# Down projection with GpSimd's transfers adding up the wide weight sum of each seven-product group

## The chip, the cores and the metric

The kernel runs on one core of one Trainium2 chip. The metric is the device time of one execution in microseconds (us), less is better. The core has TensorE (PE, matrix products into PSUM), VectorE (DVE), ScalarE (ACT), GpSimd (POOL) and SyncE (SP); SP and POOL also issue transfers between HBM and SBUF, and all transfers share 16 DMA engines.

## The reference, cut to what matters

One decoder layer on 256 tokens of width 2048: a mixing block, then a SwiGLU feed-forward block, then a final RMSNorm. The change lies in the last product, `w_down`.

```
D_MODEL = 2048
SEQ = 256
D_FF = -(-8 * D_MODEL // 768) * 256      # 5632
...
    hf = rms_norm(x, norm_ffn)
    gate, up = jnp.split(hf @ w_gu, 2, axis=-1)
    return x + (jax.nn.silu(gate) * up) @ w_down
...
    return rms_norm(x, norm_final)
```

Everything is float32.

## The kernel before, in words

**Products in three parts.** A float32 weight tile is taken as a high part (`w_hi`, rounded by ACT to the format TensorE multiplies) and a low part (`w_lo`, the rest, by DVE). Activations are kept as `actT_hi` and `actT_lo` in the same way. Each product of 128 rows by 512 columns is then three matmuls: high by high, high by low, low by high.

**The down projection.** The 5632 rows of `w_down` are 22 blocks `k` of 256 rows (`UPD`), the 2048 columns are two halves, each of a left and a right column group of 512 (`GW`). The 256 tokens are two blocks of 128. The list `DOWN`, made by `down_order()`, says in which order a half's 22 blocks are worked. A block goes in one of two ways:

- a **pair**: one unit for the left columns, one for the right. A unit is 2 token blocks by 2 row chunks by 3 matmuls, so 12 matmuls, and a pair 24;
- a **seven**: seven products of sums of the four parts of the activations with sums of the four parts of the weights stand for the eight, so 21 matmuls. It takes four slots of `w_hi` and `w_lo`: the left weights (2 products), one row chunk of the right weights (1 product), the **wide weight sum** (2 products, 1024 columns wide) and the second sum, which DVE adds up in `act_tok` from the wide one (2 products).

`SUMMED` (9) blocks of each half are sevens, those with even `k`; the others are pairs between them. The last two blocks of half 0 and the last three (`LAST`) of half 1 are worked as all their left units, then all their right units.

**Slots and who waits for whom.** `raw` (the loaded weights), `w_hi` and `w_lo` have `R` = 4 slots each. SP loads into a slot of `raw` once DVE has made the low part of what stood there (`lo_ready`). ACT writes a slot of `w_hi` once PE has used the unit four slots earlier (`unit_used`), DVE then writes the same slot of `w_lo`, and PE starts the unit at `lo_ready`. Every engine works its own list strictly in order; the order of `DOWN` sets them all.

**Names that the prediction uses.** On DVE: `down_low` makes `w_lo` from `raw` (L1269), `sum_low` makes it from a sum (L1275); `weight_sums` makes the wide sum in `gate_s` (L1287, 128x1024) and then the second sum in two steps (L1291, L1293, 128x512); `act_low` (L1096) finishes the last activations. After the last seven of a half, `fold_banks` (L1313 to L1320) and `fold_sums` (L1326 to L1328) add the banks of the shared products into the residual `x1`: `fold_banks` waits until PE is done with that seven, and is called behind the low part of the second item after it (`after == 2`), `fold_sums` behind that of the third. At the start of half 1, `down_add` (L1257) adds the two left banks of half 0 ahead of the low part of the seven's second slot, and the two right banks behind the low part of its wide sum; PE may not start that seven's third product (`product(2, s4, ...)`) before the first of the two right banks has been added (`residual_added`).

On POOL: after the last feed-forward unit it loads the kept residual back (L430, `x_kept`, 2 transfers of 1024 KB) and the row of the final norm (L431, `nf_row`, 1024 KB).

## Time and profile before

| | |
|---|---|
| median of 3 runs | 1103.7 us (1103.67 to 1104.84) |
| profiled execution, its own time | 1104.13 us |
| its span in the trace | 1102.4 us |
| TensorE busy | 1090.8 us, 99% of the span |
| VectorE busy | 863.6 us, 78% |
| ScalarE busy | 580.9 us, 53% |
| GpSimd busy | 41.3 us, 4% |
| chain that ended last | PE 96%, DVE 2%, issue 1%, DMA 1% |
| moved by DMA | 215.31 MB, mean 195 GB/s |

The trace's span begins at the first recorded instruction and leaves out what lies around it; that is the difference between the span and the execution's own time. The down projection lies between about 865 us and the end. A matmul's row shows 0.39 us, but matmuls are pipelined and start one behind another in less than that, so their pace is read from the start times.

### The profile page before, as it was taken

Reading aid. Unit: us, or ns where it says so; the run is one execution under the profiler, and the core shown is the slowest. Engines: PE = TensorE matmul, PEld = TensorE weight load, DVE = VectorE, ACT = ScalarE, POOL = GpSimd, SP = SyncE. Lnnn points to the kernel's source line nnn. Section 1 sums busy time; section 2 is a strip of 40 time slices with the busy share of each in tenths; the row PEclk is TensorE's granted clock in tenths of the full one; section 3 lists DMA queues with packets and bytes.
Section 4 is the critical chain, followed back from the end, with each engine's and each line's share of the span. In section 5 each row is a group of like instructions: output and inputs, shape, how many; then the busy total and the mean of one; then the engine's idle time right before and its main releaser. Section 6 shows DMA issues by size and latency. Waiting matters only on the chain.

```text
span 1102.4 us, 13887 instructions
## 1 busy us (share of the span) xinstructions
PE 1090.8 (99%) x5097; PEld 907.1 (82%) x5097; DVE 863.6 (78%) x1059; ACT 580.9 (53%) x704; POOL 41.3 (4%) x68
## 2 busy tenths in 40 slices
PE   9999999999999999999999999999999999999997
PEld 7797889888888888888888888888888888888885
DVE  5556866688756557988988889889888899899896
ACT  5655545555545444645545545446455556546553
POOL 2600000000010000000000000000000000000000
PEclk9999999999999999999999999999999999999999
DMA  8665646565546575656557557566566766666663
GB/s 283 212 201 171 179 134 180 160 172 153 187 176 224 178 263 175 211 170 213 197 162 230 165 177 241 173 194 209 170 212 194 282 206 213 199 199 210 201 224 115
DMA packets 110925, 215.31 MB, mean 195 GB/s; under 512 B 6940, under 2 KB 11616, under 8 KB 109984
## 3 DMA queue, kind: packets, MB, share of 16 engines
q1 hardware_dynamic: 108960, 205.36, 59.3%
q0 software_dynamic: 1632, 8.96, 2.2%
q8 instruction: 28, 0.46, 0.2%
q10 hardware_dynamic: 288, 0.39, 0.1%
q14 instruction: 17, 0.14, 0.0%
HBM read 210.49 MB, written 4.19 MB: 195 GB/s over the span
## 4 chain that ended last, share of the span: by engine, by line
PE 96%; DVE 2%; issue 1%; DMA 1%; ACT 0%; SPq 0%; POOLq 0%; POOL 0%; ACTq 0%; DVEq 0%
PE acc L1398 11%; PE acc L1400 11%; PE acc L1399 11%; PE acc L1669 11%; PE acc L1670 11%; PE acc L1671 11%; PE acc L1734 5%; PE acc L1735 5%; PE acc L1736 5%; PE mx L1390 2%; PE mx L1669 2%; PE mx L1670 2%; PE mx L1671 2%; PE mx L1734 1%; PE mx L1735 1%; PE mx L1736 1%
## 5 line engine op out<-in xcount | busy, mean ns | idle before, releaser
L749 DVE TENSOR_TENSOR w_lo<-raw,w_hi 128x1024 fp32r<-128x1024 f32 (+2 forms) x144 | 166.5, 1168 | 119.0 <-ACT w_hi L450 118.3
L450 ACT ACTIVATE w_hi<-raw 128x1024 fp32r<-128x1024 f32 (+2 forms) x144 | 144.5, 1014 | 136.1 <-PE acc L1400 130.9
L638 ACT ACTIVATE w_hi<-raw 128x1024 fp32r<-128x1024 f32 (+1 forms) x160 | 158.5, 1005 | 96.2 <-PE acc L1671 78.6
L1669 PE MATMUL acc<-w_hi,hT_hi 128*128 128x512 f32 x520 | 203.4, 391 | 0.0
L1169 DVE TENSOR_TENSOR w_lo<-raw,w_hi 128x1024 fp32r<-128x1024 f32 (+1 forms) x160 | 180.6, 1155 | 29.0 <-ACT w_hi L638 27.2
L1670 PE MATMUL acc<-w_lo,hT_hi 128*128 128x512 f32 x520 | 202.4, 389 | 0.0
L1671 PE MATMUL acc<-w_hi,hT_lo 128*128 128x512 f32 x520 | 202.3, 389 | 0.0
L1398 PE MATMUL acc<-w_hi,hT_hi 128*128 128x512 f32 (+2 forms) x444 | 169.1, 381 | 0.4 <-DVE w_lo L749 0.4
L1400 PE MATMUL acc<-w_hi,hT_lo 128*128 128x512 f32 (+2 forms) x444 | 166.4, 375 | 0.0
L1399 PE MATMUL acc<-w_lo,hT_hi 128*128 128x512 f32 (+2 forms) x444 | 166.3, 375 | 0.0
L1671 PEld LDWEIGHTS acc<-w_hi,hT_lo 128*128 128x128 f32 x520 | 97.6, 188 | 20.5
L1669 PEld LDWEIGHTS acc<-w_hi,hT_hi 128*128 128x128 f32 x520 | 97.6, 188 | 20.1
L1670 PEld LDWEIGHTS acc<-w_lo,hT_hi 128*128 128x128 f32 x520 | 97.7, 188 | 20.0
L682 ACT ACTIVATE w_hi<-raw 128x1024 fp32r<-128x1024 f32 x88 | 83.2, 969 | 34.1 <-PE acc L1736 25.5
L1269 DVE TENSOR_TENSOR w_lo<-raw,w_hi 128x1024 fp32r<-128x1024 f32 x88 | 94.5, 1111 | 6.0 <-ACT w_hi L682 3.9
L1736 PE MATMUL acc<-w_hi,actT_lo 128*128 128x512 f32 x250 | 97.3, 389 | 0.0
L1398 PEld LDWEIGHTS acc<-w_hi,hT_hi 128*128 128x128 f32 x444 | 83.4, 188 | 16.1 <-issue 0.9
L1400 PEld LDWEIGHTS acc<-w_hi,hT_lo 128*128 128x128 f32 x444 | 83.4, 188 | 15.2
L1399 PEld LDWEIGHTS acc<-w_lo,hT_hi 128*128 128x128 f32 x444 | 83.4, 188 | 14.0
L1734 PE MATMUL acc<-w_hi,actT_hi 128*128 128x512 f32 x232 | 90.5, 390 | 0.0
L1735 PE MATMUL acc<-w_lo,actT_hi 128*128 128x512 f32 x232 | 90.3, 389 | 0.0
L644 ACT ACTIVATE w_hi<-ff_sum 128x1024 fp32r<-128x1024 f32 x40 | 42.5, 1063 | 74.6 <-PE acc L1671 59.6
(296 smaller groups left out, 1512.5 us busy)
## 6 DMA issues: line engine op xcount, KB each, us to landing
raw<-in_w_gu SPq DMA_DIRECT2D x176, 512.0 KB, 4.1
raw<-in_w_down SPq DMA_DIRECT2D x88, 512.0 KB, 4.6
raw<-in_w_in SPq DMA_DIRECT2D x80, 512.0 KB, 3.9
raw<-in_w_out SPq DMA_DIRECT2D x32, 512.0 KB, 4.2
raw<-in_w_in SPq DMA_DIRECT2D x8, 272.0 KB, 2.9
raw<-in_w_in SPq DMA_DIRECT2D x8, 264.0 KB, 2.8
x<-in_x POOLq DMA_DIRECT2D x2, 1024.0 KB, 7.5
x_kept<-x POOLq DMA_DIRECT2D x2, 1024.0 KB, 6.5
```

The costliest lines, as they stand in the source:

```text
L638: act.activation(w_hi[:, v % R, c0:UC * GW], raw[:, i % R, c0:UC * GW], ACT.Copy).then_inc(hi_ready, 1)
L749: dve.tensor_tensor(w_lo[:, slot, 0:UC * width], raw[:, slot, 0:UC * width], w_hi[:, slot, 0:UC * width].bitcast(F32), ALU.subtract).then_ ...
L1169: dve.tensor_tensor(w_lo[:, v % R, c0:UC * GW], raw[:, i % R, c0:UC * GW], w_hi[:, v % R, c0:UC * GW].bitcast(F32), ALU.subtract).then_inc ...
L1398: pe.matmul(o, hi[:, c + i, tb], wh, start=first and i == 0, stop=False)
L1399: pe.matmul(o, hi[:, c + i, tb], wl, start=False, stop=False)
L1400: ins = pe.matmul(o, lo[:, c + i, tb], wh, start=False, stop=last and i == UC - 1)
L1669: pe.matmul(o, a[0], w[0], start=first, stop=False)
L1670: pe.matmul(o, a[0], w[1], start=False, stop=False)
L1671: return pe.matmul(o, a[1], w[0], start=False, stop=last)
L1734: pe.matmul(o, a[0], w[0], start=first, stop=False)
L1735: pe.matmul(o, a[0], w[1], start=False, stop=False)
L1736: return pe.matmul(o, a[1], w[0], start=False, stop=last)
```

## The change

Four things change together.

1. The wide weight sum is no longer made by DVE. `column_sums(i)` on POOL issues two plain transfers of one row chunk of the right columns into both halves of a tile, waits for them, and issues two accumulating transfers which add the left columns and the other row chunk onto them (4 transfers of 256 KB for each seven). Two tiles (`junk_f`, `gate_s`) take turns. The sum for seven `i` may begin when DVE has made the low part of the wide sum of seven `i - 2`; DVE's `weight_sums` of seven `i` waits for `d_summed`. The first two sums are issued ahead of the residual and the norm row.
2. The sums that can be made by adding alone have the right columns' sign turned, so the right columns' results are accumulated negated: ACT writes their high part with a scale of -1, DVE their low part with one scalar_tensor_tensor (`negated_low`), and the additions into the residual become subtractions.
3. Ten blocks of each half are sevens, not nine. At one place in each half (`ADJACENT`) two sevens follow each other with no pair between, and the pair between the last seven and the single units is gone in half 0 (in half 1 one of two pairs).
4. Of a seven's right weights only the row chunk that is used is loaded into `raw` (`load_lower`, 256 KB for 512 KB). The scratch of the squares and of the folds moves to `up_s`; `ident` moves behind the other tiles.

```diff
-SUMMED = 9
+SUMMED = 10
+ADJACENT = (6, 5)
...
-        between = odd[len(lead):len(lead) + SUMMED - 1]
+        between = odd[len(lead):len(lead) + 8]
...
             groups.append(("seven", 2 * i))
-            if i < SUMMED - 1:
-                groups.append(("pair", between[i]))
+            if i != ADJACENT[half] and between:
+                groups.append(("pair", between.pop(0)))
...
+            def load_lower(n, k, q):
+                sp.wait_ge(lo_ready, SLOT_OF.get(q - R, V_DN + q - R - U_DN) + 1)
+                sp.dma_start(raw[:, q % R, GW:2 * GW],
+                             w_down[(UC * k + 1) * P:(UC * k + 2) * P, n * GW:(n + 1) * GW]).then_inc(loaded[q % R], 16)
...
+            def column_sums(i):
+
+                half, k = SUM_GROUPS[i][0:2]
+                rows = [w_down[(UC * k + r) * P:(UC * k + r + 1) * P, :] for r in range(UC)]
+                left, right = (slice((2 * half + c) * GW, (2 * half + c + 1) * GW) for c in range(2))
+                tile = sum_tile(i)
+                for c in range(2):
+                    pool.dma_start(tile[:, c, :], rows[0][:, right]).then_inc(sem("d_loaded"), 16)
+                pool.wait_ge(sem("d_loaded"), 32 * (i + 1))
+                for c, src in enumerate((rows[0][:, left], rows[1][:, right])):
+                    pool.dma_start(tile[:, c, :], src, accum_op=ALU.add).then_inc(sem(f"d_summed{i % 2}"), 16)
+
             pool.wait_ge(unit_used, V_DN)
+            column_sums(0)
+            pool.wait_ge(sem("act_ready"), 2 * NG_FF)
+            column_sums(1)
             pool.wait_ge(sem("gate_used"), 2 * NG_FF)
             pool.wait_ge(sem("x1_stored"), 16 * NB)
             for b in range(NB):
                 pool.dma_start(x1[:, b, :], x1_kept[b * P:(b + 1) * P, :]).then_inc(sem("x1_back"), 16)
             pool.dma_start(nf_row[:, :], norm_final.partition_broadcast(P)).then_inc(sem("nf_loaded"), 16)
+            for i in range(2, len(SUM_GROUPS)):
+                pool.wait_ge(lo_ready, SUM_GROUPS[i - 2][2] + 3)
+                column_sums(i)
...
+            def negated_low(v, q):
+
+                dve.wait_ge(hi_ready, v + 1)
+                dve.scalar_tensor_tensor(out=w_lo[:, v % R, :], in0=raw[:, q % R, :], scalar=-1.0,
+                                         in1=w_hi[:, v % R, :].bitcast(F32), op0=ALU.mult, op1=ALU.subtract)\
+                   .then_inc(lo_ready, 1)
...
-                dve.tensor_tensor(gate_s[:, :, :], raw[:, a + 1, :].rearrange("p (k n) -> p k n", k=UC),
-                                  raw[:, a:a + 2, 0:GW], ALU.subtract).then_inc(sem("w_sums"), 1)
-                dve.wait_ge(sem("actT_psum"), NG_FF)
-                dve.wait_ge(sem("w_sums"), made - 1)
-                step(dve.tensor_tensor(act_tok[:, 0, :], raw[:, a + 1, GW:2 * GW], gate_s[:, 0, :], ALU.subtract))
+                dve.wait_ge(sem(f"d_summed{i % 2}"), 32 * (i // 2 + 1))
+                step(dve.tensor_tensor(act_tok[:, 0, :], raw[:, a + 1, GW:2 * GW], d[:, 0, :], ALU.add))
                 settle()
-                dve.tensor_tensor(act_tok[:, 1, :], raw[:, a, GW:2 * GW], act_tok[:, 0, :], ALU.subtract)\
+                dve.tensor_tensor(act_tok[:, 1, :], raw[:, a, GW:2 * GW], act_tok[:, 0, :], ALU.add)\
                    .then_inc(sem("w_sums"), 1)
...
             with dve.Fori(2, SUMMED + 1) as j:
                 gate_up(j)
-            gate_up(SUMMED + 1, summed=False)
```

How DVE's list changes at the turn from half 0 to half 1. Before, from the low part of the last seven's second sum up to the first seven of half 1 and its four `down_add`:

```order
457 L1275 TENSOR_TENSOR w_lo<-act_tok,w_hi 128x1024
458 L1269 TENSOR_TENSOR w_lo<-raw,w_hi 128x1024 x3
459 L1313 COPY gate_s<-mx 128x512
...
465 L1269 TENSOR_TENSOR w_lo<-raw,w_hi 128x1024
466 L1326 TENSOR_TENSOR x<-x,gate_s 128x512
...
469 L1269 TENSOR_TENSOR w_lo<-raw,w_hi 128x1024 x2
470 L1287 TENSOR_TENSOR gate_s<-raw 128x1024
471 L1291 TENSOR_TENSOR act_tok<-raw,gate_s 128x512
...
474 L1257 TENSOR_TENSOR x<-acc,x 128x512 x2
```

And of the change, from the first step of `fold_banks` (L1351) on; ahead of it stand two low parts, not three:

```order
436 L1351 COPY up_s<-mx 128x512
...
442 L1308 SCALAR_TENSOR_TENSOR w_lo<-raw,w_hi 128x1024
443 L1364 TENSOR_TENSOR x<-x,up_s 128x512
...
446 L1308 SCALAR_TENSOR_TENSOR w_lo<-raw,w_hi 128x1024
447 L1327 TENSOR_TENSOR act_tok<-raw,junk_f 128x512
448 L1329 TENSOR_TENSOR act_tok<-raw,act_tok 128x512
449 L1302 TENSOR_TENSOR w_lo<-raw,w_hi 128x1024
450 L1289 TENSOR_TENSOR x<-x,acc 128x512 x2
451 L1302 TENSOR_TENSOR w_lo<-raw,w_hi 128x512
452 L1315 TENSOR_TENSOR w_lo<-junk_f,w_hi 128x1024
453 L1289 TENSOR_TENSOR x<-x,acc 128x512 x2
```

Between the folds and the seven there is one low part less and no wide subtraction; PE has four units to work there, not six.

Where two sevens follow each other (shown in half 0), DVE's list in the change has the second sum of the later seven right behind the last low part of the earlier:

```order
493 L1315 TENSOR_TENSOR w_lo<-gate_s,w_hi 128x1024
494 L1315 TENSOR_TENSOR w_lo<-act_tok,w_hi 128x1024
495 L1327 TENSOR_TENSOR act_tok<-raw,junk_f 128x512
496 L1329 TENSOR_TENSOR act_tok<-raw,act_tok 128x512
497 L1302 TENSOR_TENSOR w_lo<-raw,w_hi 128x1024
498 L1302 TENSOR_TENSOR w_lo<-raw,w_hi 128x512
```

Before, two low parts of a pair stood between the second and the third of these rows at every seven.

POOL's list in the change, from the residual's storing on; before, L457's and L458's transfers followed it directly:

```order
63 L436 DMA x_kept<-x 128x2048 x2
64 L445 DMA junk_f<-in_w_down 128x512 x2
65 L448 DMA junk_f<-in_w_down 128x512 x2
66 L445 DMA gate_s<-in_w_down 128x512 x2
67 L448 DMA gate_s<-in_w_down 128x512 x2
68 L457 DMA x<-x_kept 128x2048 x2
69 L458 DMA nf_row<-in_norm_final 128x2048
70 L445 DMA junk_f<-in_w_down 128x512 x2
71 L448 DMA junk_f<-in_w_down 128x512 x2
```

Eight transfers are put ahead of the three old ones, and the third seven's sum stands behind them.

## Rows read from the trace of the kernel before

**Rows 1.** The page's busy times: busy us, share, instructions.

```profile
PE 1090.8 (99%) x5097; PEld 907.1 (82%) x5097; DVE 863.6 (78%) x1059; ACT 580.9 (53%) x704; POOL 41.3 (4%) x68
```

**Rows 2.** Everything PE waited for: us in total, times, longest.

```profile
PE acc L1441 <- POOL ident L359: 1.6, 1, 1.6
PE mx L1390 <- DMA tok<-in_x: 1.1, 1, 1.1
PE acc L1398 <- DVE w_lo L749: 0.4, 1, 0.4
PE acc L1734 <- DVE x L1257: 0.3, 1, 0.3
```

**Rows 3.** Windows: length, busy us of PE, PEld, DVE, ACT, POOL; clock, DMA share, GB/s.

```profile
870.00:876.00 6.00, 6.00 (x32) 5.08 (x31) 5.86 (x8) 3.55 (x4) 0.00 (x0) 1.00 1.01 419
876.00:960.00 84.00, 84.00 (x371) 69.15 (x371) 76.78 (x81) 49.36 (x55) 0.00 (x0) 1.00 0.65 211
```

**Rows 4.** PE's timeline (start, us): first matmuls of two pairs, one seven between.

```profile
984.53 0.39 PE L1734 MATMUL acc<-w_hi,actT_hi 128*128 128x512 f32 x1
...
994.73 0.39 PE L1734 MATMUL acc<-w_hi,actT_hi 128*128 128x512 f32 x1
```

**Rows 5.** POOL's timeline when the down projection begins.

```profile
865.42 1.06 POOL L430 DMA_DIRECT2D x<-x_kept  x2 [463.45 <-PE acc L1671]
```

**Rows 6.** DVE's timeline ahead of the first seven, and a wide scalar_tensor_tensor (grouped).

```profile
871.63 1.22 DVE L1287 TENSOR_TENSOR gate_s<-raw 128x1024 f32<-128x1024 f32 x1
872.95 0.69 DVE L1291 TENSOR_TENSOR act_tok<-raw,gate_s 128x512 f32<-128x512 f32 x1
...
874.28 1.22 DVE L1096 TENSOR_TENSOR actT_lo<-mx,actT_hi 128x1024 fp32r<-128x1024 f32 x1
875.42 1.82 DVE L1269 TENSOR_TENSOR w_lo<-raw,w_hi 128x1024 fp32r<-128x1024 f32 x2
...
L953 DVE SCALAR_TENSOR_TENSOR qT<-gwork,qT 96x1024 f32<-96x1024 f32 x1 | 1.2, 1215 | 0.0
```

**Rows 7.** PE's timeline: first matmul of the first seven.

```profile
876.95 0.39 PE L1734 MATMUL mx<-w_hi,actT_hi 128*128 128x512 f32 x1
```

**Rows 8.** DMA issues: count, KB each, median us from issue to landing.

```profile
raw<-in_w_down SPq DMA_DIRECT2D x88, 512.0 KB, 4.6
...
x_kept<-x POOLq DMA_DIRECT2D x2, 1024.0 KB, 6.5
...
nf_row<-in_norm_final POOLq DMA_DIRECT2D x1, 1024.0 KB, 12.5
...
x<-in_sgu_w POOLq DMA_DIRECT2D x1, 256.0 KB, 4.0
```

**Rows 9.** DVE's timeline at the turn of the halves.

```profile
964.96 0.68 DVE L1313 COPY gate_s<-mx 128x512 f32<-128x512 f32 x1
...
971.86 2.36 DVE L1269 TENSOR_TENSOR w_lo<-raw,w_hi 128x1024 fp32r<-128x1024 f32 x2
974.14 1.22 DVE L1287 TENSOR_TENSOR gate_s<-raw 128x1024 f32<-128x1024 f32 x1
...
980.86 1.28 DVE L1257 TENSOR_TENSOR x<-acc,x 128x512 f32<-128x512 f32 x2
```

**Rows 10.** PE's timeline at the turn of the halves.

```profile
963.59 0.39 PE L1734 MATMUL acc<-w_hi,actT_hi 128*128 128x512 f32 x1
...
981.05 0.39 PE L1736 MATMUL acc<-w_hi,actT_lo 128*128 128x512 f32 x1
981.69 0.47 PE L1734 MATMUL acc<-w_hi,s_hi 128*128 128x512 f32 x1 [0.26 <-DVE x L1257]
```

**Rows 11.** ACT's timeline at the turn of the halves.

```profile
963.85 1.06 ACT L682 ACTIVATE w_hi<-raw 128x1024 fp32r<-128x1024 f32 x1 [0.30 <-PE acc L1736]
```

**Rows 12.** PE's timeline: first matmul of the second seven of half 1.

```profile
990.65 0.39 PE L1734 MATMUL mx<-w_hi,actT_hi 128*128 128x512 f32 x1
```

**Rows 13.** DVE's timeline: low parts of that seven's wide and second sums.

```profile
989.86 1.22 DVE L1275 TENSOR_TENSOR w_lo<-gate_s,w_hi 128x1024 fp32r<-128x1024 f32 x1
992.00 1.23 DVE L1275 TENSOR_TENSOR w_lo<-act_tok,w_hi 128x1024 fp32r<-128x1024 f32 x1 [0.92 <-ACT w_hi L688]
```

**Rows 14.** DVE's groups from 870 us on: the wide subtractions (mean ns; idle before).

```profile
L1287 DVE TENSOR_TENSOR gate_s<-raw 128x1024 f32<-128x1024 f32 x18 | 22.0, 1220 | 1.2 <-DMA raw<-in_w_down 1.2
```

More of the change, by code:

```diff
@@ L123 @@
 LAST_SEVEN = [max(i for i, d in enumerate(DOWN) if d[0] == "seven" and d[1] == h) for h in range(2)]
+SUM_GROUPS = [(d[1], d[2], d[4]) for d in DOWN if d[0] == "seven"]
 FIRST_RIGHT = [i for i, d in enumerate(DOWN) if d[1] == 1][0]
@@ L203, in hybrid_layer @@
         early.close()
-        late = ExitStack()
-        actT_hi = sb("actT_hi", [P, FC, T], F32R, late, align=1024)
-        actT_lo = sb("actT_lo", [P, FC, T], F32R, late, align=1024)
-        gate_s = sb("gate_s", [P, NB, GW], where=late)
-        act_tok = sb("act_tok", [P, NB, GW], where=late)
-        s_lo = sb("s_lo", [P, SUMMED, 2, P], F32R, late, align=512)
-        up_s = sb("up_s", [P, NB, GW], where=late)
-        late.close()
         plain = ExitStack()
@@ L220, in hybrid_layer @@
         plain.close()
+        actT_hi = sb("actT_hi", [P, FC, T], F32R, align=1024)
+        actT_lo = sb("actT_lo", [P, FC, T], F32R, align=1024)
+        gate_s = sb("gate_s", [P, NB, GW])
+        act_tok = sb("act_tok", [P, NB, GW])
+        s_lo = sb("s_lo", [P, SUMMED, 2, P], F32R, align=512)
+        up_s = sb("up_s", [P, NB, GW])
+        ident = sb("ident", [P, P])
         xin = tok[:, :, :].rearrange("p b n -> p (b n)")[:, 0:NB * D].rearrange("p (b n) -> p b n", b=NB)
@@ L242, in a21, with sum_tile @@
             return t[:, 0:4 * SUMMED, :].rearrange("p (g c) t -> p g c t", c=4)[:, g0:g1, 0, P:2 * P]
+        junk_sq = up_s[:, 0, :]
+        def sum_tile(i):
+            return junk_f[:, :].rearrange("p (c n) -> p c n", c=2) if i % 2 == 0 else gate_s
         def summands(g0, g1):
@@ L669, in down_square @@
                 act.wait_ge(sem("residual_added"), 2 * NG_OUT + 2 * n + b + 1)
-                act.activation(junk_f[:, 0:GW], x1[:, b, n * GW:(n + 1) * GW], ACT.Square,
+                act.activation(junk_sq, x1[:, b, n * GW:(n + 1) * GW], ACT.Square,
                                accum_out=ss_f[:, b * NG_DN + n:b * NG_DN + n + 1]).then_inc(sem("f_squared"), 1)
@@ L676, in down_squares, with down_high, sum_high @@
                     down_square(n, b)
-            def down_high(v, q, c0=0):
+            def down_high(v, q, c0=0, sign=1.0):
                 act.wait_ge(loaded[q % R], 16 * (q // R + 1))
                 act.wait_ge(unit_used, v - R + 1)
-                act.activation(w_hi[:, v % R, c0:UC * GW], raw[:, q % R, c0:UC * GW], ACT.Copy).then_inc(hi_ready, 1)
-            def sum_high(v, src, made):
-                act.wait_ge(sem("w_sums"), made)
+                act.activation(w_hi[:, v % R, c0:UC * GW], raw[:, q % R, c0:UC * GW], ACT.Copy, scale=sign)\
+                   .then_inc(hi_ready, 1)
+            def sum_high(v, src, made, count):
+                act.wait_ge(made, count)
                 act.wait_ge(unit_used, v - R + 1)
@@ L698, in _ @@
             for i, (kind, half, k, q, v) in enumerate(DOWN):
-                down_high(v, q)
+                down_high(v, q, sign=-1.0 if kind == "right" else 1.0)
                 if kind == "pair":
-                    down_high(v + 1, q + 1)
+                    down_high(v + 1, q + 1, sign=-1.0)
                 if kind == "seven":
@@ L704, in _ @@
                     down_high(v + 1, q + 1, GW)
-                    sum_high(v + 2, gate_s, 2 * sevens - 1)
-                    sum_high(v + 3, act_tok, 2 * sevens)
+                    sum_high(v + 2, sum_tile(sevens - 1), sem(f"d_summed{(sevens - 1) % 2}"), 32 * ((sevens + 1) // 2))
+                    sum_high(v + 3, act_tok, sem("w_sums"), sevens)
                 if i in SPLIT_AT:
@@ L1335, in _ @@
                     if sevens > 1:
-                        weight_sums(q, 2 * sevens, earlier)
+                        weight_sums(q, sevens - 1, earlier)
                     earlier = v
-                down_low(v, q)
+                if kind == "right":
+                    negated_low(v, q)
+                else:
+                    down_low(v, q)
                 if kind == "pair":
@@ L1341, in _ @@
                         activate_folded(NG_FF - 1, V_DN)
-                    down_low(v + 1, q + 1)
+                    negated_low(v + 1, q + 1)
                 if kind == "seven":
@@ L1347, in _ @@
                     down_low(v + 1, q + 1, GW)
-                    sum_low(v + 2, gate_s)
+                    sum_low(v + 2, sum_tile(sevens - 1))
                     if i == FIRST_RIGHT:
@@ L1355, in _ @@
                 if i == 1:
-                    weight_sums(q + 2, 2, None)
+                    weight_sums(q + 2, 0, None)
                     act_low(NG_FF, 4 * (NG_FF - 1))
```

38 lines of the change are left out of this document (22 added, 16 removed).

## The prediction

> **What bounds the kernel now.** I read the page's busy times first: TensorE is busy for 1090.8 of 1102.4 us, VectorE for 78% [rows 1]. The list of what PE waited for says how much a relieved helper could give back: four waits, three before the down projection, and one of 0.3 us in it, for a residual addition by DVE [rows 2]. Cut into windows, the down projection shows PE without a gap from 876 to 960 us at full granted clock, with DVE busy 76.8 of 84 us and the DMA engines 65% busy at 211 GB/s [rows 3]. So DVE is nearly full but ahead, and only three things can move the time: the number of matmuls, their pace, and new waits of PE. The pace comes from two starts: from one pair to the next, with a seven between, 45 matmuls start in 994.73 - 984.53 = 10.20 us, 0.2267 us each [rows 4]. A pair is 5.44 us, a seven 4.76 us, a single unit 2.72 us.
>
> **What is taken out.** One more block in each half goes as a seven: 3 matmuls fewer, twice, so 6 x 0.2267 = **-1.36 us**. The wide subtractions leave DVE, 18 of 1.22 us, 22 us in all [rows 14]. I count them at nothing: PE did not wait for them. In their place weight_sums waits for a transfer. The negated low parts cost what the old ones did: a scalar_tensor_tensor of 1024 columns took 1.215 us, beside 1.22 us [rows 6]. ACT's scale adds no instruction. The tenth block's activation sums are DVE work in the last feed-forward group, as in the eight groups before it, where PE never waited.
>
> **What is moved: the turn of the halves.** Let T be PE's start on the first unit after half 0's last seven; before, T = 963.59 [rows 10]. Before, six units and the seven's first two products follow, so PE is due at its third product at T + 17.68 = 981.27; it starts at 981.69, 0.42 late, because DVE's first addition of a right bank began at 980.86 and released it 0.83 later [rows 9, 10]. Now four units lie there: due at T + 4 x 2.72 + 1.36 = T + 12.24. DVE's chain to the same addition begins with fold_banks, which cannot start before PE has left the last seven; ACT was released from that at T + 0.26 [rows 11]. From fold_banks to the addition DVE took 980.86 - 964.96 = 15.90 us. Of that go one low part (971.86 to 974.14 for two, so 1.14 [rows 9]) and the wide subtraction (871.63 to 872.95, 1.32 [rows 6]): 13.44 us. The third product starts at T + 0.26 + 13.44 + 0.83 = T + 14.53, 2.29 late where it was 0.42 late: **+1.87 us**. This holds any smaller wait of right unit 21 ahead of it, since DVE's chain is the longer. Behind the waiting matmul stands PE's whole list; nothing gives the time back. In half 1 a pair is still between seven and single units, which is half 0's old shape less one unit; DVE's low parts stay ahead there, and the tail is untouched.
>
> **Two sevens in a row.** DVE writes the second sum into act_tok, which it shares by all sevens, so it can begin for the later seven only behind the low part of the earlier's second sum. That started at 992.00 for a seven that PE began at 990.65, 1.35 after it, because ACT waits there for a slot, not because DVE was late [rows 12, 13]. Then: this low part 1.14, the two narrow additions 1.33 (872.95 to 874.28 [rows 6]), the next low part 1.22: 5.04 us after the seven's start, where PE is due after 4.76. 0.28 late, twice: **+0.56 us**. Before, 5.44 us of a pair lay between.
>
> **The new wait: is the first sum there in time?** POOL was released at 865.42 [rows 5] and would issue the first sum then. A POOL transfer takes 0.53 to issue (1.06 for two [rows 5]). DVE's chain from the old start of weight_sums was 1.32 + 1.33, act_low 1.14 (874.28 to 875.42), low part 1.22, end 876.64, and PE started at 876.95 [rows 6, 7]. Without the wide subtraction, weight_sums may start as late as 876.95 - 1.33 - 1.14 - 1.22 = 873.26, so the sum must land within **7.8 us**. It is two transfer pairs one behind the other. The trace has no accumulating transfer and no plain pair of 256 KB. One plain POOL transfer of 256 KB landed 4.0 us after issue, a pair of 1024 KB in 6.5 [rows 8]. For the accumulating pair the lower end is the plain one (4.0), the upper twice it (8.0); nothing suggests less, as the same bytes come from HBM. I take 4.0 and one more pass over the pair's 0.52 MB at the 419 GB/s that the full queues showed [rows 3], 5.2. Then 0.53 + 4.0 + 0.53 + 5.2 = 10.3, the sum is there at 875.7, PE starts at 875.7 + 1.33 + 1.14 + 1.22 = 879.4: **+2.4 us**. At the ends: 9.1 us, +1.2; and 13.1 us, +5.2.
>
> The Trainium skill ("DMA: Bandwidth & Descriptors", section on the SWDGE path) gives about 2.0 us plus bytes / 436 GB/s per POOL transfer. By it the pair of 1024 KB would take 6.8, and the trace agrees with 6.5; the single 256 KB would take 2.6, the row says 4.0. By the page a pair of 256 KB takes 3.2 and the sum 2 x 3.2 + 1.06 = 7.5 us, just in time, and this term is nil. The same page (rules for kernel authors) says that an accumulating transfer reads its destination and writes it later, which no run here has shown yet; it speaks for my extra pass.
>
> **Queued behind it.** The second sum is issued at about 871 and due 10.2 us of PE after the first: hidden. Then come x_kept's return and nf_row, which once took 12.5 us to land [rows 8]; issued at 878.2 now, landed at 890.7. Their own users come much later (folds near 960). But the third sum's loads stand behind them in POOL's queue: landed near 892.0, accumulated by 897.7. Due: PE reaches the third seven at 876.95 + 20.4 + 2.4 = 899.8, less 2.6 for sum and low part, 897.2. **+0.5 us**, at the ends 0 and 3. Later sums: tile free 0.4 after a seven's start (989.86 + 1.22, against 990.65 [rows 12, 13]), needed two periods of 10.2 later less 2.6: 17.4 us for 10.3. Around two sevens in a row 12 us: still hidden at 10.3, about 1 us late each at 13.1.
>
> **Traffic.** For each seven and pair the loads were 2.10 MB in 10.2 us, 206 GB/s, as the row says (211 [rows 3]). Now 1.84 for raw and 1.05 for the sums: 283 GB/s, or 334 if accumulating reads twice, against 419 when full. SP's loads (4.6 us to landing [rows 8]) may lengthen, but DVE frees their slots earlier than before by its 1.3 us per seven. Nil, with an end of +2.
>
> **The sum.** -1.36 + 1.87 + 0.56 + 2.4 + 0.5 = **+4.0 us**. The profiled execution took 1104.13, 0.4 above the median of the three runs; on the median this makes **1107.7 us**.
>
> **Rivals.**
> - *The first sums come in time* (within about 8.5 us). For it: the page's formula, and the pair of 1024 KB at 6.5. Against: 4.0 for a single 256 KB, and two dependent steps. Then -1.36 + 1.87 + 0.56 = +1.1, **1104.8**, no measurable change. It decides at a column sum of 8.9 us: above that the whole is over +2.2.
> - *The sums are late at every seven.* An accumulating transfer far slower than twice a plain one, so that a sum takes over 17.4 us. At 19 us it is 1.6 x 18 later, with 10 at the start: about **1140**. For it: no row shows such a transfer. Against: bytes and engines have room.
> - *PE's pace quickens when DVE has less to do.* 1% on 996 matmuls is -2.3 us: with sums in time 1102.5, and if the turn did not stall at all (-1.87 - 0.42) 1100.2. It would have to come to over 1.5% alone, or with the turn. Against: the pace of 0.2267 was read where DVE is as full as elsewhere, and no row ties the two. This is the faster side.
> - *DVE's relief pays.* It would have to be in waits of PE, and there were 0.3 us.
>
> **How the numbers follow.** No change is told from a change up to about 0.2% here (2.2 us). My forecast, with the turn, the neighbours and late first sums: 0.62, slower. Sums in time: 0.29, same. Late everywhere: 0.06, slower. Faster pace: 0.03. The range goes down to just under the second case, 1104.3, and up to where an accumulating pair of nearly 8 us puts it (+1.1 + 5.2 + 3 = +9.3): 1113.0.
>
> **What would show it.** PE's waits should now name DVE at four places: near 877 (its releaser a DMA into junk_f behind it, some 2.4 us), near 897, at the turn (2 us, the same addition of x) and at the two neighbouring sevens (0.3 each). A column sum from its first issue to landing near 10 us. Six matmuls fewer. If PE has no wait near 877, the sum was quick; if the turn shows under 1 us, the chain from fold_banks is not what releases it.

## The result, and the profile after

The change takes **1146.6 us** (median of 4 runs, 1146.0 to 1150.6) against 1103.8 before: ratio 1.0394, interval 1.0369 to 1.0418. The forecast was 1107.7 (1104.3 to 1113.0): the sign was right, the size wrong by more than a factor of ten. The case that I had given 0.06, sums late at every seven with about 1140 us, is the nearest in time; only part of its mechanism came, as shown below.

The page: busy times, two DMA queues of the whole run, and the engines' shares of the chain that ended last.

```profile
PE 1105.5 (97%) x5091; PEld 913.9 (80%) x5091; DVE 849.9 (74%) x1054; ACT 583.7 (51%) x708; POOL 99.8 (9%) x148
q1 hardware_dynamic: 106400, 200.12, 55.0%
q0 software_dynamic: 10592, 29.94, 10.4%
PE 77%; DMA 13%; DVE 6%; issue 1%; POOL 1%; ACT 1%; SPq 0%; POOLq 0%; DVEq 0%; ACTq 0%
```

Six matmuls fewer than in [rows 1], as forecast, and yet PE is busy 14.7 us longer; and the chain, 1% DMA before, is now 13% DMA. What PE waited for (us in total, times, longest), the down projection's two rows:

```profile
PE mx L1775 <- DVE w_lo L1302: 24.4, 11, 4.8
PE acc L1775 <- DVE x L1289: 1.7, 1, 1.7
```

26.1 us of waits where [rows 2] had 0.3. With the 14.7 us of busy time they make 40.5 of the span's 41.8 us (1144.2 - 1102.4). Windows of the down projection (columns as in [rows 3]):

```profile
880.00:900.00 20.00, 13.55 (x46) 10.69 (x47) 10.91 (x13) 6.87 (x7) 4.50 (x7) 0.78 0.85 301
900.00:920.00 20.00, 20.00 (x79) 16.27 (x78) 13.81 (x15) 10.03 (x12) 5.83 (x8) 0.88 0.93 240
...
1020.00:1040.00 20.00, 19.80 (x88) 16.04 (x87) 14.75 (x17) 12.81 (x16) 5.40 (x8) 1.00 0.97 288
1060.00:1080.00 20.00, 14.80 (x52) 11.29 (x51) 13.24 (x14) 9.03 (x10) 5.89 (x8) 0.83 0.78 211
```

From 880 us on the DMA share is 0.78 to 0.97 where it was 0.65, and PE has gaps all along, not just at the start. The longer busy time is the clock's. From 900 to 920 us PE is busy throughout but starts 79 matmuls where 88 would fit at 0.2267 us each: the granted clock is 0.88. PE's timeline behind a wait shows how:

```profile
969.79 0.80 PE L1775 MATMUL mx<-w_hi,actT_hi 128*128 128x512 f32 x1 [4.63 <-DVE w_lo L1302]
970.38 0.63 PE L1776 MATMUL mx<-w_lo,actT_hi 128*128 128x512 f32 x1
970.81 0.63 PE L1777 MATMUL mx<-w_hi,actT_lo 128*128 128x512 f32 x1
...
973.95 0.39 PE L1777 MATMUL mx<-w_hi,s_lo 128*128 128x512 f32 x1
974.18 0.39 PE L1775 MATMUL mx<-w_hi,s_hi 128*128 128x512 f32 x1
```

After 4.6 us without work the matmuls start 0.43 us apart, which is the level of 1.2 GHz, and at 973.95 they are 0.23 apart again, that of 2.4 GHz. A long wait is paid for twice. The trace's clock record has five stretches at the lower level between 880 and 1079 us, 27.3 us in all; four of them begin within waits of 4.0 to 4.8 us, the fifth 0.9 us behind one of 1.9. Half of 27.3 is 13.7 us, nearly all of the 14.7.

**The first seven.** DVE's timeline; its rows before are [rows 6]:

```profile
871.43 0.82 DVE L1336 TENSOR_TENSOR actT_lo<-actT_lo,s_hi 128x640 fp32r<-128x640 f32 x1
878.75 0.69 DVE L1327 TENSOR_TENSOR act_tok<-raw,junk_f 128x512 f32<-128x512 f32 x1 [6.50 <-DMA junk_f<-in_w_down]
```

and POOL's timeline, the first, the third and the fifth sum (the same tile `junk_f`; a pair of loads at L445, a pair of accumulating transfers at L448):

```profile
865.96 1.09 POOL L445 DMA_DIRECT2D junk_f<-in_w_down  x2 [463.70 <-PE acc L1712]
872.45 1.83 POOL L448 DMA_DIRECT2D junk_f<-in_w_down  x2 [5.40 <-DMA junk_f<-in_w_down]
...
884.47 1.08 POOL L445 DMA_DIRECT2D junk_f<-in_w_down  x2 [0.84 <-DVE w_lo L1315]
900.09 1.80 POOL L448 DMA_DIRECT2D junk_f<-in_w_down  x2 [14.53 <-DMA junk_f<-in_w_down]
...
913.07 1.12 POOL L445 DMA_DIRECT2D junk_f<-in_w_down  x2 [1.08 <-DVE w_lo L1315]
922.15 1.81 POOL L448 DMA_DIRECT2D junk_f<-in_w_down  x2 [7.96 <-DMA junk_f<-in_w_down]
```

The first sum took 878.75 - 865.96 = 12.8 us, 6.5 for the loads and 6.3 for the accumulating pair; I had forecast 10.3. The fifth needed 9.1 us for its loads alone. A pair of accumulating transfers occupies POOL for 1.8 us, 0.9 each, where a plain one takes the 0.53 of [rows 5].

**The later sevens.** A piece of the chain that ended last, its longest members (start, us, what):

```profile
909.90 1.75 DVE w_lo L1302 x2
911.66 8.90 DMA raw<-in_w_down
...
920.79 0.70 DVE act_tok L1327
921.51 0.69 DVE act_tok L1329
922.21 1.75 DVE w_lo L1302 x2
923.97 9.04 DMA raw<-in_w_down
```

A loop of 12.3 us (909.90 to 922.21): a slot's low part releases SP's load into it, the load takes 9 us to land, the second sum needs what it brought (1.4), then the low parts (1.8). Before, the same loop was 4.6 for the load [rows 8], 2.6 for `weight_sums` and 1.8 for two low parts [rows 6], 9.0 us, beside PE's 10.2 for a seven and a pair [rows 4]. It had 1.2 us of room, which the forecast never worked out. A second loop was over the period too: POOL takes one sum at a time, 9.1 us until a pair of loads is there and 1.8 to issue the accumulating pair, 10.9 us. At 15 of the 20 sums, though, what it waited for last was DVE's release of the tile.

What DVE waited for at its 20 second sums (us in total, times, longest):

```profile
DVE act_tok L1327 <- DMA raw<-in_w_down: 34.7, 10, 7.7
DVE act_tok L1327 <- DMA junk_f<-in_w_down: 19.0, 6, 6.5
DVE act_tok L1327 <- DMA gate_s<-in_w_down: 6.7, 2, 4.3
```

So it was SP's load at ten sevens, POOL's sum at eight, and neither at two. The page's DMA issues (columns as in [rows 8]):

```profile
raw<-in_w_down SPq DMA_DIRECT2D x68, 512.0 KB, 5.9
...
junk_f<-in_w_down POOLq DMA_DIRECT2D x40, 256.0 KB, 6.5
```

### The profile page after: what moved, and what is told of

Read it like the earlier page. It is cut to its first block, busy times and chain, and to the rows that moved or that the text cites. A ratio compares the mean times of both kernels' runs of the same rounds, so it can differ in the third digit from the quotient of the medians.

```text
span 1144.2 us, 14004 instructions
## 1 busy us (share of the span) xinstructions
PE 1105.5 (97%) x5091; PEld 913.9 (80%) x5091; DVE 849.9 (74%) x1054; ACT 583.7 (51%) x708; POOL 99.8 (9%) x148
## 4 chain that ended last, share of the span: by engine, by line
PE 77%; DMA 13%; DVE 6%; issue 1%; POOL 1%; ACT 1%; SPq 0%; POOLq 0%; DVEq 0%; ACTq 0%
PE acc L1439 11%; PE acc L1710 11%; PE acc L1441 11%; PE acc L1712 11%; PE acc L1440 11%; PE acc L1711 11%; DMA junk_f<-in_w_down 6%; DMA raw<-in_w_down 5%; PE mx L1431 2%; DVE w_lo L1302 2%; DMA gate_s<-in_w_down 2%; PE mx L1710 2%; PE mx L1711 2%; PE mx L1712 2%; PE mx L1614 1%
## 5 line engine op out<-in xcount | busy, mean ns | idle before, releaser
L1202 DVE TENSOR_TENSOR w_lo<-raw,w_hi 128x1024 fp32r<-128x1024 f32 (+1 forms) x160 | 180.5, 1154 | 28.9 <-ACT w_hi L668 27.3
L1775 PE MATMUL acc<-w_hi,actT_hi 128*128 128x512 f32 x220 | 87.1, 396 | 0.1
L1776 PE MATMUL acc<-w_lo,actT_hi 128*128 128x512 f32 x220 | 86.8, 395 | 0.0
L1302 DVE TENSOR_TENSOR w_lo<-raw,w_hi 128x1024 fp32r<-128x1024 f32 (+1 forms) x64 | 65.8, 1053 | 8.3 <-ACT w_hi L712 7.2
```

Source lines behind the costliest of these rows:

```text
L1202: dve.tensor_tensor(w_lo[:, v % R, c0:UC * GW], raw[:, i % R, c0:UC * GW], w_hi[:, v % R, c0:UC * GW].bitcast(F32), ALU.subtract).then_inc ...
L1302: dve.tensor_tensor(w_lo[:, v % R, c0:UC * GW], raw[:, q % R, c0:UC * GW], w_hi[:, v % R, c0:UC * GW].bitcast(F32), ALU.subtract).then_inc ...
```

## The experiments

Theory: the sums' transfers fill the DMA engines, SP's loads into `raw` take longer, and the slot loop exceeds PE's period; the waits for the sums add to it. Rivals: only the start costs (first sum, 3 MB burst); the two dependent steps are too long whatever their size; the order (ten sevens, neighbours, turn) costs; traffic alone does it without any wait. The kernels (the two columns on the right are those of the profiled execution; two_sums, plain, nine, traffic2, first_spread, plain_spread, every_other and unawaited ran twice each):

| kernel | us (range) | against before | PE's waits in the down projection | PE busy |
|---|---|---|---|---|
| the change | 1146.6 (1146.0–1150.6) | 1.0394 [1.0369, 1.0418] | 26.1 | 1105.5 |
| two_sums | 1119.2 (1118.9–1119.6) | 1.014 [1.011, 1.0169] | 10.5 | 1095.1 |
| plain | 1124.4 (1123.9–1124.8) | 1.0186 [1.0157, 1.0216] | 13.2 | 1094.6 |
| nine | 1136.6 (1135.0–1138.2) | 1.0297 [1.0261, 1.0332] | 21.5 | 1101.7 |
| traffic2 | 1127.0 (1126.0–1128.0) | 1.0203 [1.0163, 1.0243] | 12.2 | 1098.9 |
| order_alone | 1105.3 (1105.0–1106.2) | 1.0009 [0.9998, 1.0021] | 2.3 | 1091.6 |
| first_spread | 1140.6 (1137.5–1143.7) | 1.0326 [1.0252, 1.0401] | 22.2 | 1100.4 |
| dve_sums | 1111.0 (1110.9–1112.9) | 1.0051 [1.0032, 1.0071] | 6.8 | 1093.0 |
| thin | 1107.6 (1107.1–1108.6) | 1.0034 [1.0022, 1.0047] | 2.3 | 1091.1 |
| plain_spread | 1121.8 (1120.5–1123.1) | 1.016 [1.0131, 1.019] | 11.6 | 1093.0 |
| every_other | 1118.0 (1117.5–1118.4) | 1.0125 [1.0096, 1.0155] | 11.3 | 1094.3 |
| unawaited | 1123.0 (1121.7–1124.3) | 1.0171 [1.0141, 1.02] | 13.2 | 1095.0 |
| three_sums | 1112.5 (1109.6–1112.7) | 1.0079 [1.0062, 1.0096] | 6.3 | 1090.4 |

The kernel before took 1103.8 to 1104.5 us beside them.

### two_sums: only the first two sums

```diff
-            for i in range(2, len(SUM_GROUPS)):
-                pool.wait_ge(lo_ready, SUM_GROUPS[i - 2][2] + 3)
-                column_sums(i)
...
-                dve.wait_ge(sem(f"d_summed{i % 2}"), 32 * (i // 2 + 1))
+                dve.wait_ge(sem(f"d_summed{i % 2}"), 32)
```

> The changed kernel with POOL making only the first two column sums; the other 18 sevens read the two tiles as they then stand, so their wide sums are left out. What is left of the change is its order of work, the first sum and SP's loads. Order theory (the turn of the halves, two sevens in a row, a late first sum, as in my prediction, with the first sum's wait of 6.5 us that the trace of the change shows): 1103.8 - 1.4 + 1.9 + 0.6 + about 5 = 1110, at most 1112. If transfers are the cause of the rest, nearly all of the 43 us is gone here. If the order were the cause, it would stay above 1130.

1119.2 us, 7 above the most that I had expected. So the new order and the start cost 15 us together, and the other 27 come with the sums behind them. DVE's timeline shows the two long waits of the start:

```profile
877.06 0.69 DVE L1324 TENSOR_TENSOR act_tok<-raw,junk_f 128x512 f32<-128x512 f32 x1 [5.65 <-DMA junk_f<-in_w_down]
...
895.34 0.69 DVE L1324 TENSOR_TENSOR act_tok<-raw,gate_s 128x512 f32<-128x512 f32 x1 [7.92 <-DMA raw<-in_w_down]
```

The second is no sum: it is SP's load into `raw`, under way while POOL's queue moves `x_kept` and `nf_row` (3 MB). The load in the chain that ended last:

```profile
881.38 13.74 DMA raw<-in_w_down
```

and the queues from 881 to 896 us (packets, MB, share of 16 engines):

```profile
q0 software_dynamic: 670, 3.57, 70.0%
q1 hardware_dynamic: 839, 1.62, 28.0%
```

In order_alone below, where the 3 MB are spread out and POOL makes no sum, the load of this size in this stretch lands in 5.2 us. Both waits let the clock fall; PE starts 50 matmuls from 880 to 900 us at a granted clock of 0.76.

### plain: the same transfers, none accumulating

```diff
-                    pool.dma_start(tile[:, c, :], src, accum_op=ALU.add).then_inc(sem(f"d_summed{i % 2}"), 16)
+                    pool.dma_start(tile[:, c, :], src).then_inc(sem(f"d_summed{i % 2}"), 16)
```

> The changed kernel with the accumulating transfers made plain ones of the same size, so the wide sums are wrong and every wait, issue and byte from HBM stays. If it is the accumulation that fills the DMA engines (218 GB/s for POOL's queue against 331 for SP's in the trace of the change), loads of raw fall back from 6 to 7.6 towards 5 us and the time to 1108 to 1120. If it is the bytes and the two dependent steps alone, 1135 or more.

1124.4 us, 4 above the range that I had given to full engines. Accumulating costs 22 us over plain transfers of the same bytes. The queues from 900 to 1080 us (packets, MB, share of 16 engines), of the change and of plain:

```profile
q1 hardware_dynamic: 14285, 27.29, 45.2%
q0 software_dynamic: 6954, 16.18, 41.3%
```

```profile
q1 hardware_dynamic: 16155, 30.85, 52.5%
q0 software_dynamic: 5435, 17.81, 32.4%
```

In 180 us, POOL's queue moved 16.18 MB in 41.3% of the engines' time: 218 GB/s for each full share. Plain it is 17.81 MB in 32.4%, 305 GB/s. Half of these bytes are loads in both kernels; if those ran at 305 in the change too, the accumulating half ran at 170, which is 1.8 times a plain transfer's time on the engines. That is a low estimate. The trace's packet records of the same stretch of the change have the parts: on average an accumulating packet of 2 KB took 210 ns, SP's plain one of 2 KB 97 ns, POOL's plain one of 4 KB 167 ns. Per byte an accumulating transfer held an engine 2.2 times as long as SP's loads and 2.5 times as long as POOL's own.

### nine: the old order, nine sevens, all sums by POOL

```diff
-SUMMED = 10
-ADJACENT = (6, 5)
+SUMMED = 9
+ADJACENT = (99, 99)
...
+            gate_up(SUMMED + 1, summed=False)
```

> The changed kernel with nine sevens a half and no two in a row, the old order of blocks, all else as changed. The order theory gives -1.9 - 0.6 + 1.4 = -1 us against the change; less traffic (18 sums for 20) a few us more. Theories of traffic or chain: it stays at 1135 to 1146. If ten sevens or their neighbours were the cause: under 1115.

1136.6 us: 10 less than the change, but 33 above before. The order is not the cause; fewer sums and no neighbours give a part back.

### traffic2: all transfers, later sums not waited for

The sums from the third on go into `junk_f` and half of `nf_row`, whose own load moves behind the last sum; a tile of their own (4096 B for each partition, 480 are free) does not fit.

```diff
+        def written_tile(i):
+            wide_part = junk_f[:, :] if i % 2 == 0 else nf_row[:, 0:2 * GW]
+            return gate_s if i == 1 else wide_part.rearrange("p (c n) -> p c n", c=2)
...
-                dve.wait_ge(sem(f"d_summed{i % 2}"), 32 * (i // 2 + 1))
+                dve.wait_ge(sem(f"d_summed{i % 2}"), 32)
```

> The changed kernel with all 20 column sums issued, but those from the third on go into junk_f and into half of nf_row, which nobody reads before the norm row is loaded after the last sum; the sevens from the second on read a stale tile. The wait for the sum is left out (wide sums wrong), the traffic is kept. Between the run with two sums (1119.2) and the change (1146.6) lie 27 us. Theory of traffic (the accumulating transfers lengthen SP's loads of raw, and DVE waits for those): most of it stays, 1135 to 1146. Theory of the chain (DVE waits for the sum itself): 1119 to 1125.

1127.0 us: 8 above two_sums, 20 below the change, and between the two ranges that I had given. The traffic alone slows SP's loads (6.3 us to landing, median from 900 to 1080 us) but only the wait for the sums makes it the change's time. Neither is nearly all.

### order_alone: no sum by POOL

```diff
+BY_POOL = []
+BY_DVE = [0]
...
-            for b in range(NB):
-                pool.dma_start(x1[:, b, :], x1_kept[b * P:(b + 1) * P, :]).then_inc(sem("x1_back"), 16)
-            pool.dma_start(nf_row[:, :], norm_final.partition_broadcast(P)).then_inc(sem("nf_loaded"), 16)
             for i in range(2, len(SUM_GROUPS)):
                 pool.wait_ge(lo_ready, SUM_GROUPS[i - 2][2] + 3)
-                column_sums(i)
+                if i in BY_POOL:
+                    column_sums(i)
+                if i in (3, 5):
+                    b = (i - 3) // 2
+                    pool.dma_start(x1[:, b, :], x1_kept[b * P:(b + 1) * P, :]).then_inc(sem("x1_back"), 16)
+                if i == 7:
+                    pool.dma_start(nf_row[:, :], norm_final.partition_broadcast(P)).then_inc(sem("nf_loaded"), 16)
```

> The changed kernel without any column sum on POOL: DVE makes the first seven's wide sum from whole loads, the other 19 are left out (stale tiles); the residual's two transfers and the norm row, 3 MB in one burst before, come one at a time, behind the groups 1, 3 and 5. What is left of the change is the order of work. My recorded terms for the order: six matmuls fewer -1.4, turn of the halves +1.9, two sevens in a row +0.6: 1.1 above before. If the run with two sums owed its 15 us to the first sum and to loads of raw behind the 3 MB, this one is at 1105. If the order costs more than I worked out, it stays near 1115.

1105.3 us. It leaves out 19 of the 20 wide sums. What PE waited for in the down projection:

```profile
PE acc L1795 <- DVE x L1303: 1.7, 1, 1.7
...
PE mx L1795 <- DVE w_lo L1316: 0.6, 2, 0.3
```

DVE makes the first sum there and nobody waits for another. These rows are my turn (a wait of 1.7 where it was 0.3: my +1.87 was 1.4) and my two neighbouring sevens (0.3 each, as forecast), and nothing else.

### first_spread: the start taken away

As order_alone, but the 19 later sums by POOL (`BY_POOL = [1, 2, ... 19]`). It computes the whole reference.

> The changed kernel with the first seven's wide sum made by DVE (its weights loaded whole) and the 3 MB of residual and norm row spread behind the fourth, sixth and eighth sum; 19 column sums by POOL as changed, nothing left out. It takes away the two long stalls at the start (4 to 5 us each, and TensorE's lower clock behind them). Traffic theory: the lengthened loads at every seven stay, 1125 to 1133. If the stalls at the start had set off the lateness of the later ones, under 1115.

The two executions took 1137.5 and 1143.7 us, 3 to 9 below the change and well above the 1125 to 1133 that I had expected. Without the start's burst the lateness is made later: DVE waits 23.5 us for `raw` (9 times), 18.2 for `junk_f`, 12.0 for `gate_s`.

### dve_sums: the new order with DVE making every sum

```diff
+BY_POOL = []
+BY_DVE = [0, 1, 2, 3, 4, 5, 6, 7, 8, 9, 10, 11, 12, 13, 14, 15, 16, 17, 18, 19]
...
+                if i in BY_DVE:
...
+                    dve.tensor_tensor(d[:, :, :], raw[:, a + 1, :].rearrange("p (k n) -> p k n", k=UC),
+                                      raw[:, a:a + 2, 0:GW], ALU.add).then_inc(sem("wide_made"), 1)
```

> The changed kernel with all 20 wide sums by DVE from whole loads, as before the change, and no column sums; ten sevens a half, the new order and the negated right columns stay; nothing left out. By the chains of my prediction with 1.32 us of DVE more in each: turn of the halves 3.6 late for 0.4, two sevens in a row 1.6 late each, six matmuls fewer: 5 us above before, 1109. If the negation or the new place of the tiles costs something, it is above 1112.

1111.0 us, 2 above what I had expected. The tenth seven does not pay by itself: with DVE's wide additions in the chains of the turn and of the neighbours PE waits 6.8 us. Against order_alone it has 19 wide additions more, whole loads for them, and the 3 MB in one burst again; all of that costs 5.7 us, so in the new order sums that cost nothing could have given back no more.

### thin, plain_spread, unawaited: bytes, accumulating and waits taken apart

All three start from first_spread, so that only the steady part differs. thin cuts the bytes and keeps every step:

```diff
-                    pool.dma_start(tile[:, c, :], rows[0][:, right]).then_inc(sem("d_loaded"), 16)
+                    pool.dma_start(tile[:, c, 0:GW // 8], rows[0][:, right][:, 0:GW // 8]).then_inc(sem("d_loaded"), 16)
...
-                    pool.dma_start(tile[:, c, :], src, accum_op=ALU.add).then_inc(sem(f"d_summed{i % 2}"), 16)
+                    pool.dma_start(tile[:, c, 0:GW // 8], src[:, 0:GW // 8], accum_op=ALU.add).then_inc(sem(f"d_summed{i % 2}"), 16)
```

> The chain without the bytes. As first_spread (DVE makes the first sum, the 3 MB spread out), but each of the four transfers of a sum moves 64 of its 512 columns, so an eighth of the bytes; all steps, waits and the order stay. Leaves out: seven eighths of the columns of the 19 sums are stale. Theory (loop with 1.2 us of room, pushed over by full DMA engines: raw loads from 4.5 to 6 to 9 us, sums 16 to 18 us): the raw loads go back to 4.4 to 4.7 us, a sum takes about 2 x 2.5 + 1.5 = 6 to 8 us and the kernel 1105 to 1107, as order_alone (1105.3). Rival 1 (the two dependent steps and the issue alone are too slow, whatever their size): over 1120. Rival 2 (an accumulating transfer is slow per transfer, not per byte): over 1115 with junk_f and gate_s still over 5 us to landing.

plain_spread drops `accum_op` as plain did:

> The same bytes and steps without accumulating. As first_spread (1140.6), but the second pair of each sum overwrites and does not accumulate. Leaves out: the adding, so the sums are wrong. plain without the spreading took 1124.4 against 1146.6 of the change, 22 less; the start stalls cost 6. Theory (an accumulating transfer holds an engine about twice as long as a plain one of the same bytes, which fills the engines and delays SP's raw loads): 1110 to 1119, with raw loads of 5 to 6 us to landing. Rival (accumulating matters only through its own latency at the start): within 5 of first_spread.

unawaited writes the sums where nobody waits for them (`nf_row` is loaded behind the last one):

```diff
         def sum_tile(i):
-            return junk_f[:, :].rearrange("p (c n) -> p c n", c=2) if i % 2 == 0 else gate_s
+            return gate_s
+
+        def written_tile(i):
+            wide_part = junk_f[:, :] if i % 2 == 0 else nf_row[:, 0:2 * GW]
+            return wide_part.rearrange("p (c n) -> p c n", c=2)
```

> All the bytes, accumulating, with nobody waiting for a sum, and without the stalls at the start. As first_spread, but from the second sum on they go into junk_f and the first half of nf_row's tile (nf_row is loaded after the last), and DVE and ACT read the first sum's tile throughout, without a wait. Leaves out: all later sums are stale. traffic2 with the stalls at the start took 1127.0, and the start cost 6 to 14. Theory (full engines slow SP's raw loads and with them the slot loop, and that alone is 5 to 10 us; the wait for the sums is the rest): 1110 to 1120, PE's waits on w_lo 3 to 8 us. Rival 1 (traffic alone costs nothing in the steady state): 1105 to 1107. Rival 2 (traffic alone is nearly all): over 1130.

Over order_alone's 1105.3 us: steps and waits without bytes **+2.3** (thin); accumulating bytes without waits **+17.7** (unawaited); plain bytes with waits **+16.5** (plain_spread); accumulating bytes with waits **+35.3** (first_spread, 32.2 to 38.4 by its two executions). The chain of two steps alone does not cost what that rival said, and an accumulating transfer is not slow by the piece. Bytes and waits together cost some 15 us (12 to 18) more than one and the other. (order_alone and first_spread ran beside a kernel before of 1104.5 us, the other three beside one of 1103.8; by the ratios the three differences are 0.2 to 0.5 us larger.) thin came out 0.6 us above the range that I had given, plain_spread and unawaited 3 each: even the cheaper traffic pushes the loop over. Between plain_spread and first_spread, DVE's waits for SP's loads hardly differ (20.7 and 23.5 us), those for sums do (9.6 and 30.2). thin's waits in the down projection are the same two rows as order_alone's, and by the traces it issues its last store at 1100.0 us, order_alone at 1100.6: its 2.3 us lie behind that, 6.0 us to the end of the span for 3.9, and the steady part cost nothing. Its DMA issues from 900 to 1080 us are

```profile
raw<-in_w_down SPq DMA_DIRECT2D x53, 512.0 KB, 4.4
...
gate_s<-in_w_down POOLq DMA_DIRECT2D x32, 32.0 KB, 3.1
...
junk_f<-in_w_down POOLq DMA_DIRECT2D x30, 32.0 KB, 4.2
```

while unawaited's for `raw` is

```profile
raw<-in_w_down SPq DMA_DIRECT2D x47, 512.0 KB, 6.4
```

and the only transfer that its DVE waits for is SP's:

```profile
DVE act_tok L1352 <- DMA raw<-in_w_down: 30.8, 11, 7.6
```

That is the loop of `raw` by itself, with no sum in it. The windows from 900 to 1080 us put the three beside each other, order_alone, thin, first_spread:

```profile
900.00:1080.00 180.00, 177.66 (x780) 145.76 (x779) 148.49 (x161) 105.71 (x116) 1.06 (x2) 1.00 0.58 190
```

```profile
900.00:1080.00 180.00, 177.68 (x780) 145.75 (x779) 148.61 (x161) 105.56 (x117) 46.85 (x64) 1.00 0.68 204
```

```profile
900.00:1080.00 180.00, 158.84 (x661) 126.82 (x660) 126.02 (x137) 90.46 (x101) 46.17 (x64) 0.96 0.89 256
```

### every_other: DVE makes every second sum

`BY_POOL` has the odd sums, `BY_DVE` the even ones. It computes the whole reference.

> Half the sums by POOL. As first_spread, but DVE makes the sums 0, 2, 4 ... 18 (with whole raw loads for these) and POOL's accumulating transfers the ten others. Computes the whole reference. Theory (lateness arises where the engines stay full; between two POOL sums the loop now has 20.4 us of PE and can recover): excess over dve_sums/order_alone (1105 to 1111) far less than half of the 29 to 35 us of first_spread, 1108 to 1116. Rival (each POOL sum costs its 1.6 to 1.9 us wherever it stands): (1140.6 + 1108) / 2, about 1124.

1118.0 us, 12.6 above order_alone, where half of first_spread's excess and half of the wide additions' 5.7 would be 20.5. The cost falls faster than the number of sums, but it missed my range of 1108 to 1116 by 2.

### three_sums: POOL's sums at the three tight places alone

`BY_POOL = [7, 10, 16]`, the rest by DVE.

> Three sums by POOL, the others by DVE: the later seven of the two neighbours in each half (7 and 16) and the first of half 1 (10), the places where a wide addition by DVE stands in a chain that PE waits for; the 3 MB spread out. Computes the whole reference. All sums by DVE gave 1111.0, none 1105.3. Theory (a POOL sum costs only where the engines stay full before and behind it; alone, with two or more sevens to recover, it lands in time): 1105 to 1107.5, PE's waits the turn's 1.7 to 2.0 and under 2 besides, raw loads 4.5 to landing. Rival (each POOL sum costs 1.5 to 2 us wherever it stands): 1109 to 1111. Both say that it does not beat the kernel before (1103.8) by what can be measured.

1112.5 us: a miss; the rival's 1109 to 1111 is nearer. The profiled execution, its quickest (1109.6), shows why, in POOL's and DVE's timelines at sum 16, with no other sum of POOL's for 60 us:

```profile
1025.87 1.12 POOL L453 DMA_DIRECT2D junk_f<-in_w_down  x2 [62.05 <-DVE w_lo L1329]
1031.89 1.81 POOL L456 DMA_DIRECT2D junk_f<-in_w_down  x2 [4.90 <-DMA junk_f<-in_w_down]
...
1039.52 0.69 DVE L1347 TENSOR_TENSOR act_tok<-raw,junk_f 128x512 f32<-128x512 f32 x1 [1.79 <-DMA junk_f<-in_w_down]
```

A lone sum takes 1039.52 - 1025.87 = 13.65 us, over the 12 us that two neighbouring sevens leave, and DVE waits 1.8 us for it (2.0 at sum 7). So the two steps are too long just there, independently of other sums. I had put POOL's sums where DVE has the least time and overlooked that the transfers have the least time there too. What the other three runs added, 3 us, no view shows. No version beat the kernel before.

## Why the prediction was wrong

The traffic term leaned on the first window of [rows 3]. The queues of the kernel before in that window, 870 to 876 us (packets, MB, share of 16 engines):

```profile
q0 software_dynamic: 300, 2.20, 87.0%
q1 hardware_dynamic: 155, 0.32, 13.6%
```

Term by term:

- **Six matmuls fewer**: right, x5091 for x5097.
- **The turn and the neighbours**: right in place and kind. The turn was +1.4, not +1.87; the neighbours 0.3 each. order_alone as a whole was 0.9 above the kernel before (1105.3 beside 1104.5), where -1.36 + 1.87 + 0.56 says +1.1.
- **The first sum late (+2.4)**: right in kind, mis-sized. The sum took 12.8 us, within the 13.1 of my upper end, and PE waited 4.8 us. The term that failed is the load pair, 6.5 us with its issue for 4.5; the accumulating pair took 6.3 for 5.7. I also charged the wait at its length and not the clock behind it.
- **Queued behind it (+0.5)**: wrong. I looked for the burst's victim in POOL's own queue and found the third sum, which I had loaded near 892.0; it was loaded at 900.1. The dearer victim was the other queue: SP's load, for which DVE waited 7.7 us in the change and 7.9 in two_sums. The start as a whole cost 14 us (two_sums less order_alone), not 2.9; with all the later sums in place, taking it away gave back only 3 to 9 (first_spread).
- **Traffic (nil, with an end of +2)**: the step that failed. I compared 334 GB/s wanted with 419 seen and called the difference room. The 419 was read in one window of 6 us [rows 3], and it is not the rate of SP's loads. By the queues above it was POOL's transfers of 1 MB, 421 GB/s of a full share, that filled it. The other window of [rows 3] had the price of the loads: 211 GB/s at a share of 0.65 are 325. Against that the 283 wanted are 87% of the engines' time, and the 334 are more than all of it. Of the change, by the queues' shares from 900 to 1080 us: raw loads ran at 27.29 MB / (0.452 x 180 us) = 335 GB/s of a full share, so 1.84 MB are 5.5 us, and 1.05 MB at 218 are 4.8: 10.3 us of all engines for every 10.2 us of PE. A byte's price is not fixed (POOL's plain packets of 4 KB took 167 ns on average in the change and 213 in plain), so this is no strict bound, but there is no room in it. And "SP's loads may lengthen, but DVE frees their slots earlier" was not held against the loop's room of 1.2 us; the loads lengthened by 1.3 us in the page's median and by 4.4 in the loop shown above. Traffic without waits was +17.7.
- **"Later sums: 17.4 us for 10.3"**: wrong in both numbers. Where DVE waited for a sum behind the start, that sum took 16.1 to 18.7 us from POOL's first issue to DVE's use, and its release moves back with every delay. So the rival "late at every seven" is in part what happened: POOL's sum was late at eight sevens, though five of the six behind the start took less than its threshold of 17.4 us, and SP's load was late at ten. That its price of 1140 was near is luck: it held no wait for SP's loads, and 10 us for a start that cost 14. Nor did it need "an accumulating transfer far slower than twice a plain one": 2.2 to 2.5 times per byte was enough, on top of plain transfers that take longer to land under load. What I held against it, "bytes and engines have room", is the mistake of the point above.

By the fit of the Trainium skill ("DMA: Bandwidth & Descriptors", section on the SWDGE path) I had estimated 3.2 us for a pair of 256 KB. Even thin's pieces of 32 KB took 3.1 to 4.2 us each and the first pair of 256 KB 6.5 with its issue, so the runs disagree; that fit has no term for what else is on the engines. The Trainium skill's rules for kernel authors, in "DMA: Bandwidth & Descriptors", say that spreading transfers over the issuing engines brings no bandwidth, since all run on the same 16 engines and interleave. The trace of two_sums agrees: beside the 3 MB on POOL's queue, SP's load took 13.7 us and DVE waited 7.9 us for it.

**What stays open.** How the 24 us between unawaited and the change (18 to first_spread, which has the same start) divide into later releases, later loads and clock: the three feed each other, and no run held one still. The same holds for what accumulating adds: from plain to the change DVE's waits for SP's loads grow from 10.7 to 34.7 us and those for sums from 18.7 to 25.7, but in the pair without the start's burst nearly all of the growth is in the sums. The clock's part is bounded by PE's busy time: 14.7 us in all, of which 1105.5 - 1095.0 = 10.5 lie between the two.

## What to carry to other kernels

Before adding traffic, find each loop that runs through a transfer (slot free, load, use, slot free), add it up beside the consumer's period, and price a lengthening of that transfer against the room; here there were 1.2 us of room, and traffic that nobody waited for cost 17.7 us, while the busy engine that was being relieved had kept PE waiting for 0.3 us. Count traffic in engine time by the queues' own shares, with accumulating transfers at 2.2 to 2.5 times their bytes, and not against the highest rate seen in a short window, which here was that of other transfers. Work moved off an engine that nobody waits for buys nothing: DVE's 22 us had cost nothing in the old order and were worth at most 5.7 in the new one.

## What the runs showed of the hardware

Accumulating transfers of 128x512 held an engine 2.2 times as long per byte as SP's plain ones and 2.5 times as long as POOL's (packets of 210, 97 and, for 4 KB, 167 ns), 218 against 305 GB/s of a full share for a half-and-half mix beside an all plain one, and took 0.9 us each to issue against 0.53. POOL's transfers of 1 MB moved at 421 GB/s of a full share, SP's loads at 325 to 335. A load of 256 KB by SP took 13.7 us to land while POOL's queue held 70% of the engines' time, 5.2 without that burst. The same transfers with an eighth of the bytes cost only 2.3 us, none of it in the down projection, though POOL was busy just as long with them (46.85 us of 180 in thin, 46.17 in first_spread). After a wait of 4.6 us PE ran for 3.2 us (969.79 to 972.94) at the lower clock level, 0.43 us from one matmul to the next.
